# The state-space loop of a two-layer encoder: the first pair of the gated unit is summed whole inside it, and the block outputs share one PSUM bank

## The chip, the cores and the metric

The kernel runs on one core of a Trainium2 chip. The metric is the device time of one execution in microseconds. Before the change, three runs gave a median of 983.5 us (982.42 to 984.84). All arithmetic is float32.

## What is computed

The input is a residual stream of 256 positions by 1024 features. Two layers change it. Layer 0 has an attention and a linear recurrence side by side. Layer 1 has a state-space mixer (S5) with a gated linear unit behind it. Each layer ends in a mixture of 16 experts. The change touches only the S5 mixer of layer 1:

```python
def _s5_mixer(h, ...):
    ...
    bu_re = jnp.einsum('bsgc,gpc->bsgp', u, bb_re)          # inputs of the states
    bu_im = jnp.einsum('bsgc,gpc->bsgp', u, bb_im)
    h_re, h_im = scan(ab, bu)                               # complex diagonal recurrence over the positions
    y = C_re h_re - C_im h_im + d * u
    act = jax.nn.gelu(y.reshape(B, S, D_MODEL))
    zg = act @ glu_w + glu_b                                # (256, 1024) @ (1024, 2048)
    return zg[..., :D_MODEL] * jax.nn.sigmoid(zg[..., D_MODEL:])   # value * sigmoid(gate)

x = x + g_m * m                                             # then norm, router, experts
```

## The kernel before, in words

There are five streams of instructions: TensorE (PE), VectorE (DVE), ScalarE (ACT), GpSimd (POOL), and SyncE (SP), which starts the large transfers. They are held together by counting semaphores. The order on each engine is written out by hand, so an instruction that waits holds back all that stand behind it on its engine. PSUM has 8 banks of 128 by 512 float32, `bank[0]` to `bank[7]`.

**The state-space loop** (PE lines 1843 to 1859, DVE lines 1270 to 1296, ACT lines 840 to 848) runs over `KD` = 8 blocks k of 128 features, and is unrolled. In one turn:

- `states(k + 1)` on PE multiplies the next block's features into the state inputs (L1801, 32 matmuls, banks 0 to 3). It waits until VectorE has read those banks for block k (`s_used`).
- VectorE reads the four banks for block k and turns them by a rotation table (L1277 to L1280), adds (L1282, L1283), does eight scans (L1287), and turns back (L1292 to L1295). The last of these signals `q_ready`. It then takes the next block, for which it waits on `s5_ps`, the signal of `states`.
- `ada(16 + k, 17 + k)` on PE (L1347) multiplies one of eight 2 MB units of the layer's conditioning weights into bank 7. SyncE loads them alternately into ring slots 0 and 1, each when the unit two before it has been used (L350).
- From k = 2 on, `glu_blocks` (L1838) adds to the gated unit what the finished block k - 1 of `actT` gives.
- `outputs(k)` on PE adds up block k of y: the d term (L1815), the direct term (L1816), and, when `q_ready` is k + 1, 64 matmuls from the states (L1823). It signals `y5_ps`.
- ScalarE applies the gelu to it (L842), writes `actT[:, k]`, signals `act_ready`, and makes a later diagonal (L834).

**The gated unit.** The product `act @ glu_w` is cut into eight tiles of 128 positions by 512 columns. A pair m (`GLU_PAIRS`, a column half h and a position half b) consists of a value tile (part 0) and a gate tile (part 1) over the same positions and columns. Each tile is a bias matmul (`glu_bias`, L1830) and 8 block matmuls of 128x128 by 128x512 (`glu_blocks(m, part, lo, hi)`, L1838, blocks lo to hi - 1). Its weights are one of four 2 MB units (`s5_glu_w`, number 2 h + part). Pairs 0 and 1 both use units 0 and 1, pairs 2 and 3 use units 2 and 3.

Before the change the tiles are placed so. The value tile of pair 0 grows inside the loop in bank 6. In the last turn (k = 7) the gate tile of pair 0 is begun in bank 0, with bias and 3 blocks, ahead of `outputs(7)`; 4 more blocks follow behind it, then `ada_cols(2)` (L1357). With block 7 the two tiles of pair 0 are ended. After `gate_row(2)` (L1382) come pairs 1, 2 and 3, each with two whole tiles.

For each pair ScalarE takes the sigmoid of the gate tile (L851), and VectorE multiplies and adds to x (L1302, L1304, L1305). After pair 3 the norm of the mixture of experts begins (L888, L612), its transposes (L1322), router and gathers (L1577), and then four groups of four experts.

**Loads.** SyncE sends, in this order: the rotation tables into slots 4 and 5, conditioning units 16 and 17, gated-unit weights 0 and 1 (L337) into slots 2 and 3, conditioning units 18 to 23, then gated-unit weight 2 (after `q_ready` 4) and weight 3 (after `q_ready` 8), which take the places of the rotation tables. Then it sends the experts' weights of layer 1 (L341), each when its slot's last reader has signalled. For the slots of the gated unit's weights that is the end of a tile of pair 1 (`glu_ps` 3 and 4) or of pair 3 (`glu_ps` 7 and 8).

Of the kernel before, what the change touches and what calls it, by code (L numbers as in the profile page):

```python
# [22 lines left out]
T = 256  # L23
NB = T // P
KD = D // P
# [60 lines left out]
class Chain:  # L86
# [5 lines left out]
    def link(self, ins):  # L92
        ins.then_inc(self.sem, 1)
        self.n += 1
        self.eng.wait_ge(self.sem, self.off + self.n)
# [9 lines left out]
def build(nc, a, out):  # L105
    ctx = ExitStack()
    with ctx:
        def sb(name, shape, dt=F32):
            return ctx.enter_context(nc.sbuf_tensor(name, shape, dt))
# [3 lines left out]
        def S(name):  # L113
            if name not in sems:
                sems[name] = ctx.enter_context(nc.semaphore(name))
            return sems[name]
# [7 lines left out]
        grow = sb("grow", [P, D])  # L124
# [21 lines left out]
        bank = [PS[:, i, :] for i in range(8)]  # L146

        def w3(off, *dims):

            n = 1  # L150
            for d in dims:
                n *= d
            v = work[:, off:off + n]
            if len(dims) == 1:
                return v
            names = " ".join("abcd"[:len(dims)])
            return v.rearrange(f"p ({names}) -> p {names}", **dict(zip("abcd", dims)))
# [41 lines left out]
        gfrow = w3(o, D); o += D  # L199
# [65 lines left out]
                  (1, 0, 1, 4), (1, 1, 1, 5), (0, 0, 1, 7), (0, 1, 1, 4))  # L265
        K0_BANK = (3, 6)
        GLU_PAIRS = ((0, 0), (0, 1), (1, 0), (1, 1))
        GLU_BANK = ((6, 0), (1, 2), (3, 7), (4, 5))

        BATCHES = ((0, ADA_FIRST), (ADA_FIRST, ADA_EARLY), (ADA_EARLY, ADA_ALL))  # L270
        arows = (arow0, arow0, arow1)
# [19 lines left out]
        def loaded(eng, n, i=None):  # L291

            v = 16 * (n // SLOTS + 1)
            if n >= MOE_BASE[1] and (n - ADA_BASE) % SLOTS < 2:
                v -= 16
            eng.wait_ge(S(f"loaded{n % SLOTS}"), v if i is None else v + i * (16 * PER_GROUP // SLOTS))

        def u3(n, c=HALF):
            return ring[:, n % SLOTS, :].rearrange("p (k c) -> p k c", c=c)
# [279 lines left out]
        def _(act):  # L579
# [11 lines left out]
            for name, (at, n) in ROWS.items():  # L591
                dst = rows[at:at + n, :]
# [31 lines left out]

            def gate_row(n):
                act.wait_ge(S("grow_ps"), n + 1)
                at, row = (4, grow) if n % 2 == 0 else (2, gfrow)
                s.activation(row[:, 0:HALF], bank[at], ACT.Copy)
                s.activation(row[:, HALF:], bank[at + 1], ACT.Copy).then_inc(S("grow_ready"), 1)

# [7 lines left out]
            def rows_out(i):  # L638

                act.wait_ge(S("ada_used"), BATCHES[i][1])  # L640
                s.activation(arows[i], bank[7], ACT.Copy).then_inc(S("ada_rows"), 1)
# [188 lines left out]
            def diagonal(k):  # L830

                if k >= 2:
                    act.wait_ge(S("y5_ps"), k - 1)
                s.activation(diagD[:, k % 2, :], ident[:, :], ACT.Copy, scale=col("s5d", k)).then_inc(  # L834
                    S("diag_ready"), 1)
# [4 lines left out]
            for k in range(KD):  # L840
                act.wait_ge(S("y5_ps"), k + 1)
                s.activation(actT[:, k, :].rearrange("p (j l) -> p l j", l=2),  # L842
                             bank[4 + k % 2][:, 0:T].rearrange("p (l j) -> p l j", l=2),
                             ACT.Gelu_apprx_tanh).then_inc(S("act_ready"), 1)
                if k + 2 < KD:
                    diagonal(k + 2)
                if k == KD - 2:
                    rows_out(2)
            for m, (h, b) in enumerate(GLU_PAIRS):
                act.wait_ge(S("glu_ps"), 2 * m + 2)  # L850
                s.activation(q_a[:, m, :], bank[GLU_BANK[m][1]], ACT.Sigmoid).then_inc(S("glu_sig"), 1)  # L851
                if m == 0:
                    gate_row(2)
# [9 lines left out]
        def _(dve):  # L863
# [436 lines left out]
            for m, (h, b) in enumerate(GLU_PAIRS):  # L1300
                dve.wait_ge(S("glu_sig"), m + 1)
                link(v.tensor_tensor(q_a[:, m, :], q_a[:, m, :], bank[GLU_BANK[m][0]], ALU.mult))  # L1302
                dve.wait_ge(S("grow_ready"), 3)
# [13 lines left out]
        def _(pe):  # L1317
# [6 lines left out]
            def bcol(ap, n=P):  # L1324
                return ap.to_broadcast([ap.shape[0], n])
# [25 lines left out]
            def ada_cols(i):  # L1351

                pe.wait_ge(S("ada_rows"), i + 1)
                lo, hi = BATCHES[i]
                n, r = hi - lo, lo % ADA_EARLY
                for c4 in range(4):
                    last = mm(bank[6 if i == 0 else 7][:, c4 * n:(c4 + 1) * n], arows[i][:, c4 * P:(c4 + 1) * P],  # L1357
                              sel[:, r:r + n], start=True, stop=True)
                last.then_inc(S("ada_cols_ps"), 1)
# [16 lines left out]
            def gate_row(n):  # L1376

                L, sec = n // 2, (G_M if n % 2 == 0 else G_F)
                pe.wait_ge(S("mod_cols"), (2, 2, 3, 3)[n])
                at = 4 if n % 2 == 0 else 2  # L1380
                for k in range(KD):
                    last = mm(bank[at + k // 4][:, (k % 4) * P:(k % 4 + 1) * P], bcol(mod[:, L, sec, k:k + 1]),  # L1382
                              ident[:, :], start=True, stop=True)
                last.then_inc(S("grow_ps"), 1)
# [29 lines left out]
            for j in range(LT):  # L1414
                at = 768 + j * P
# [7 lines left out]
            for j in range(LT):  # L1423
                at = 1280 + j * P
# [30 lines left out]
            for b in range(NB):  # L1455
                n_k = P * (b + 1)
                for i in range(4):
                    for r in range(2):
                        h = 2 * i + r
                        if b == 0:  # L1460
                            dst = PS[:, r, i * P:(i + 1) * P]
                        else:
                            dst = PS[:, (4, 2)[r] + i // 2, (i % 2) * T:(i % 2 + 1) * T]
# [341 lines left out]
            def outputs(k):  # L1805

                m = k % 2
                dst = bank[4 + m]
                pe.wait_ge(S("diag_ready"), k + 1)
                if k >= 2:  # L1810
                    pe.wait_ge(S("act_ready"), k - 1)
                else:
                    pe.wait_ge(S("tab_evac"), 12)
                    pe.wait_ge(S("k0_evac"), 2)
                mm(dst[:, 0:T], diagD[:, m, :], hT[:, k, :].rearrange("p (j l) -> p l j", l=2), start=True, stop=False)  # L1815
                mm(dst[:, 0:NJ], K0[:, k, :], hT[:, k, 0::2], start=False, stop=False)  # L1816
                pe.wait_ge(S("q_ready"), k + 1)
                for w in range(4):
                    for l, tab in ((1, H1), (0, H0)):
                        n = NJ - 1 + l  # L1820
                        for q4 in range(4):
                            cc = slice(32 * q4, 32 * q4 + 32)
                            last = mm(dst[cc, NJ:T] if l else dst[cc, 1:NJ], tab[:, w // 2, k, cc],  # L1823
                                      qq[m][:, w, q4 * NJ:q4 * NJ + n], start=False, stop=w == 3 and l == 0)
                last.then_inc(S("y5_ps"), 1)

            def glu_bias(m, part):

                r = GLU_PAIRS[m][0] + 2 * part
                mm(bank[GLU_BANK[m][part]], bcol(ident[0:4, r:r + 1]), glub, start=True, stop=False)  # L1830

            def glu_blocks(m, part, lo, hi):

                h, b = GLU_PAIRS[m]
                n = GLU_BASE + 2 * h + part
                loaded(pe, n)
                for k in range(lo, hi):
                    last = mm(bank[GLU_BANK[m][part]], actT[:, k, b * P:(b + 1) * P], u3(n)[:, k, :], start=False,  # L1838
                              stop=k == KD - 1)
                if hi == KD:  # L1840
                    last.then_inc(S("glu_ps"), 1)
# [3 lines left out]
            for k in range(KD):  # L1845
                if k + 1 < KD:
                    states(k + 1)
                ada(ADA_EARLY + k, ADA_EARLY + k + 1)
                if k == 2:
                    pe.wait_ge(S("glub_in"), 16)  # L1850
                    glu_bias(0, 0)
                if k >= 2:
                    pe.wait_ge(S("act_ready"), k)
                    glu_blocks(0, 0, 0 if k == 2 else k - 1, k)
                if k == KD - 1:
                    pe.wait_ge(S("s_used"), KD)
                    glu_bias(0, 1)
                    glu_blocks(0, 1, 0, 3)
                outputs(k)
            glu_blocks(0, 1, 3, KD - 1)  # L1860
            ada_cols(2)
            pe.wait_ge(S("act_ready"), KD)
            glu_blocks(0, 0, KD - 1, KD)
            glu_blocks(0, 1, KD - 1, KD)
            gate_row(2)
            for m in range(1, 4):
                if m == 3:
                    pe.wait_ge(S("grow_ready"), 3)
                for part in range(2):
                    glu_bias(m, part)  # L1870
                    glu_blocks(m, part, 0, KD)
            pe.wait_ge(S("x_new"), 3)
# [27 lines left out]
```

## Time and profile before

| | us |
|---|---|
| Median of 3 runs | 983.5 |
| The profiled execution, device time | 982.88 |
| Its span | 981.1 |
| TensorE busy | 848.6 (86%) |
| VectorE busy | 304.4 (31%) |
| ScalarE busy | 192.7 (20%) |
| GpSimd busy | 150.6 (15%) |
| State-space loop, from the first L1277 to the last L1295 | 494.9 to 567.2 |
| Gated unit after the loop, to the last sigmoid | 567.4 to 626.7 |

The span is the time from the first to the last instruction that the profile shows. In the rows below, PE is TensorE's matmuls and PEld its weight loads, which overlap them. A float32 matmul appears as two records, so "x16" at L1838 is 8 block matmuls. A row of the timeline says when the group began, how long it took, engine, line and operation, what it writes and reads, how many, and in brackets how long the engine had been idle before it and what ended that.

### The profile page before, as it was taken

To read this page: it belongs to the slowest core of one execution; us is meant where nothing else is said; L and a number is where in the kernel's file an instruction comes from. 1 tells how busy PE (TensorE), PEld (TensorE's weight loads), DVE (VectorE), ACT (ScalarE), POOL (GpSimd) and SP (SyncE) were. 2 spreads that over 40 slices of the span, in tenths; PEclk is the share of its full clock that TensorE was granted. 3 is DMA by queue.
4 is the path that set the end of the run, shared out by engine and by line. 5 is a ranking of instruction groups with operands and counts; after the bars stand their busy time and mean duration, and the time that the engine had idled before them with its cause. 6 is when DMAs were issued, how large, how long until landed. Compare 5 with 4: busy or idle time off the path is not lost.

```text
span 981.1 us, 12755 instructions
## 1 busy us (share of the span) xinstructions
PE 848.6 (86%) x5229; PEld 463.8 (47%) x5230; DVE 304.4 (31%) x708; ACT 192.7 (20%) x311; POOL 150.6 (15%) x244
## 2 busy tenths in 40 slices
PE   3799566979999999899868799789999799999993
PEld 0367352456546455365444454344444464554641
DVE  1320653254113141031389921332000121311314
ACT  1301224042121131121320010211000211312211
POOL 3201002708543434600000000010000000000000
PEclk9799867989999999999999999979999899999997
DMA  9999697533999999999698674404777289999961
GB/s 311 347 382 290 242 358 283 163 113 142 398 393 399 399 396 395 399 391 398 257 387 286 242 276 152 172 1 155 274 257 257 87 326 396 392 399 390 395 267 65
DMA packets 126288, 285.32 MB, mean 291 GB/s; under 512 B 7093, under 2 KB 8389, under 8 KB 125993
## 3 DMA queue, kind: packets, MB, share of 16 engines
q1 hardware_dynamic: 119392, 276.83, 76.7%
q0 software_dynamic: 1984, 5.21, 1.8%
q10 hardware_dynamic: 4872, 2.72, 1.1%
q8 instruction: 29, 0.48, 0.2%
q14 instruction: 11, 0.08, 0.0%
HBM read 279.50 MB, written 5.24 MB: 290 GB/s over the span
## 4 chain that ended last, share of the span: by engine, by line
PE 70%; DVE 12%; DMA 9%; ACT 3%; issue 3%; SPq 2%; DVEq 0%; ACTq 0%
PE PS L1550 17%; PE PS L1569 12%; PE PS L1577 8%; PE PS L1593 7%; PE PS L1553 6%; PE PS L1838 5%; DMA ring<-in_moe_w 5%; PE PS L1322 4%; PE PS L1518 3%; PE PS L1411 3%; DMA work<-in_ada_w 2%; DMA ring<-in_ada_w 2%; DVE work L1287 2%; PE PS L1347 2%; SPq L350 1%
## 5 line engine op out<-in xcount | busy, mean ns | idle before, releaser
L1569 PE MATMUL PS<-ring,work 128*64 128x512 f32 (+1 forms) x512 | 130.5, 597 | 6.2 <-ACT work L768 6.2
L1550 PE MATMUL PS<-ring,hT 128*64 128x256 f32 x896 | 107.5, 381 | 3.7 <-DMA ring<-in_moe_w 3.7
L1550 PE MATMUL PS<-ring,yg 128*64 128x256 f32 x896 | 106.6, 379 | 0.0
L1550 PEld LDWEIGHTS PS<-ring,hT 128*64 128x64 f32 x896 | 66.1, 137 | 41.2 <-issue 7.9
L1569 PEld LDWEIGHTS PS<-ring,work 128*64 128x64 f32 (+1 forms) x512 | 43.1, 143 | 85.4 <-issue 83.9
L1209 DVE TENSOR_TENSOR work<-work,PS 128x512 f32<-128x512 f32 x32 | 22.0, 688 | 194.3 <-PE PS L1550 146.4
L1577 PE MATMUL PS<-work,xhat 128*128 128x256 f32 (+1 forms) x256 | 76.2, 449 | 6.7 <-issue 6.6
L1550 PEld LDWEIGHTS PS<-ring,yg 128*64 128x64 f32 x896 | 67.6, 137 | 29.1
L1213 DVE COPY yg<-PS 128x512 f32<-128x512 f32 x32 | 22.1, 692 | 180.5 <-PE PS L1569 180.5
L1593 PE MATMUL PS<-yg,grow 64*128 64x512 f32 (+1 forms) x256 | 70.1, 612 | 7.1 <-DVE yg L1213 7.1
L1577 PEld LDWEIGHTS PS<-work,xhat 128*128 128x128 f32 x256 | 48.4, 204 | 38.6 <-issue 21.9
L1838 PE MATMUL PS<-ring,yg 128*128 128x512 f32 x128 | 58.9, 604 | 0.0
L1347 PE MATMUL PS<-ring,condz 128*32 128x512 f32 x320 | 41.7, 650 | 14.0 <-DMA ring<-in_ada_w 13.8
L772 ACT ACTIVATE yg<-PS 128x512 f32<-128x512 f32 x32 | 19.1, 597 | 166.5 <-PE PS L1569 166.5
L1593 PEld LDWEIGHTS PS<-yg,grow 64*128 64x128 f32 (+1 forms) x256 | 25.6, 186 | 35.9 <-issue 22.1
L764 ACT ACTIVATE work<-PS 128x512 f32<-128x512 f32 x32 | 19.1, 598 | 104.6 <-PE PS L1550 79.3
L493 POOL TENSOR_SCALAR rt<-rt 128x4 f32<-128x4 f32 x2 | 0.5, 241 | 253.3 <-DVE rti L1170 253.3
L1838 PEld LDWEIGHTS PS<-ring,yg 128*128 128x128 f32 x128 | 23.1, 189 | 33.9 <-issue 33.9
L768 ACT ACTIVATE work<-PS 128x512 f32<-128x512 f32 x32 | 19.1, 597 | 96.4 <-PE PS L1322 96.4
L1322 PE MATMUL PS<-ident,work 128*128 128x128 f32 x176 | 29.3, 288 | 6.7 <-ACT yg L772 6.3
L1518 PE MATMUL PS<-ring,yg 128*128 128x512 f32 x64 | 29.9, 628 | 2.8 <-issue 2.8
L1322 PEld LDWEIGHTS PS<-ident,work 128*128 128x128 f32 x176 | 19.2, 143 | 27.5 <-issue 26.8
(348 smaller groups left out, 968.5 us busy)
## 6 DMA issues: line engine op xcount, KB each, us to landing
ring<-in_moe_w SPq DMA_DIRECT2D x96, 2048.0 KB, 16.5
ring<-in_ada_w SPq DMA_DIRECT2D x20, 2048.0 KB, 14.9
work<-in_ada_w SPq DMA_DIRECT2D x4, 2048.0 KB, 17.1
ring<-in_s_glu_w SPq DMA_DIRECT2D x4, 2048.0 KB, 16.7
ring<-in_ab_w_in SPq DMA_DIRECT2D x3, 2048.0 KB, 22.1
ring<-in_ab_w_out SPq DMA_DIRECT2D x2, 2048.0 KB, 10.0
rot_tables<-work POOLq DMA_DIRECT2D x16, 256.0 KB, 5.8
ring<-rot_tables SPq DMA_DIRECT2D x2, 2048.0 KB, 10.9
```

Of the source, the lines that this page charges most:

```text
L1209: v.tensor_tensor(he[:, e % 2, :], he[:, e % 2, :], bank[1], ALU.mult).then_inc(S("he_ready"), 1)
L1213: v.tensor_copy(yg[:, e % 2, HALF:], bank[3]).then_inc(S("y_dve"), 1)
L1322: return nc.tensor.transpose(dst, src, ident[0:n, 0:n])
L1347: last = mm(bank[7][32 * j:32 * j + 32, :], condz[:, k, 32 - r:64 - r], ada_unit(u)[:, k, :], start=any(first) and k < 4, stop=any(final) ...
L1411: last = mm(dst, w[:, k, :], hT[:, k, :], start=k == 0, stop=k == KD - 1)
L1518: last = mm(bank[2 * b + h], mixT[:, k, b * P:(b + 1) * P], u3(N_WIN + h)[:, k, :], start=k == 0, stop=k == KD - 1)
L1550: last = mm(dst[64 * u:64 * u + 64, 0:256], hg[k][:, e * P:e * P + 64], w[:, k, 256 * u:256 * u + 256], start=k == 0, stop=k == KD - 1)
L1553: last = mm(dst, hg[k][:, e * P:(e + 1) * P], w[:, k, :], start=k == 0, stop=k == KD - 1)
L1569: last = mm(dst, heT[:, at:at + (64 if narrow else P)], w[:, c4, h * HALF:(h + 1) * HALF], start=c4 == 0, stop=c4 == KF - 1)
L1577: last = mm(bank[k % 2].rearrange("p (e n) -> p e n", n=P)[:, :, 0:n_s], xhat[:, b, k * P:(k + 1) * P], pick[:, b, :, 0:n_s], start=b == 0 ...
L1593: last = mm(acc[2 * b + h], pickT[pp, e, b * P:(b + 1) * P], yg[pp, at, h * HALF:(h + 1) * HALF], start=False, stop=False)
L1838: last = mm(bank[GLU_BANK[m][part]], actT[:, k, b * P:(b + 1) * P], u3(n)[:, k, :], start=False, stop=k == KD - 1)
```

## The change

The value and gate tiles of pair 0 are now both summed inside the loop, in banks 6 and 5. In the last turn, where the gate tile of pair 0 was begun, the value tile of pair 1 is begun (bank 0), with bias and 3 blocks, and 4 blocks behind `outputs(7)`. After the loop, block 7 ends three tiles (both of pair 0, the value tile of pair 1). Of pair 1 only the gate tile is left to do whole.

To free bank 5, all blocks' outputs go to bank 4 (before: banks 4 and 5 in turn). So `outputs(k)` waits for the gelu of block k - 1 (before: k - 2). The banks of the other tiles, and those of the gate row after the loop (2 and 3 instead of 4 and 5), are moved to suit.

```diff
-        GLU_BANK = ((6, 0), (1, 2), (3, 7), (4, 5))
+        GLU_BANK = ((6, 5), (0, 1), (7, 4), (2, 3))
...
             def gate_row(n):
...
-                at, row = (4, grow) if n % 2 == 0 else (2, gfrow)
+                at, row = 4 if n == 0 else 2, grow if n % 2 == 0 else gfrow
...
                 s.activation(actT[:, k, :].rearrange("p (j l) -> p l j", l=2),
-                             bank[4 + k % 2][:, 0:T].rearrange("p (l j) -> p l j", l=2),
+                             bank[4][:, 0:T].rearrange("p (l j) -> p l j", l=2),
...
-                at = 4 if n % 2 == 0 else 2
+                at = 4 if n == 0 else 2
                 for k in range(KD):
                     last = mm(bank[at + k // 4][:, (k % 4) * P:(k % 4 + 1) * P], bcol(mod[:, L, sec, k:k + 1]),
...
             def outputs(k):
                 m = k % 2
-                dst = bank[4 + m]
+                dst = bank[4]
                 pe.wait_ge(S("diag_ready"), k + 1)
-                if k >= 2:
-                    pe.wait_ge(S("act_ready"), k - 1)
+                if k:
+                    pe.wait_ge(S("act_ready"), k)
...
                 if k == 2:
                     pe.wait_ge(S("glub_in"), 16)
                     glu_bias(0, 0)
+                    glu_bias(0, 1)
                 if k >= 2:
                     pe.wait_ge(S("act_ready"), k)
-                    glu_blocks(0, 0, 0 if k == 2 else k - 1, k)
+                    for part in range(2):
+                        glu_blocks(0, part, 0 if k == 2 else k - 1, k)
                 if k == KD - 1:
                     pe.wait_ge(S("s_used"), KD)
-                    glu_bias(0, 1)
-                    glu_blocks(0, 1, 0, 3)
+                    glu_bias(1, 0)
+                    glu_blocks(1, 0, 0, 3)
                 outputs(k)
-            glu_blocks(0, 1, 3, KD - 1)
+            glu_blocks(1, 0, 3, KD - 1)
             ada_cols(2)
             pe.wait_ge(S("act_ready"), KD)
-            glu_blocks(0, 0, KD - 1, KD)
-            glu_blocks(0, 1, KD - 1, KD)
+            for part in range(2):
+                glu_blocks(0, part, KD - 1, KD)
+            glu_blocks(1, 0, KD - 1, KD)
             gate_row(2)
             for m in range(1, 4):
                 if m == 3:
                     pe.wait_ge(S("grow_ready"), 3)
-                for part in range(2):
+                for part in range(1 if m == 1 else 0, 2):
                     glu_bias(m, part)
                     glu_blocks(m, part, 0, KD)
```

## Rows read from the trace of the kernel before

**Rows 1.** The page's first line.

```profile
span 981.1 us, 12755 instructions
```

**Rows 2.** The chain that ended last, 460 to 650 us: start, duration, engine, line.

```profile
549.20 0.69 DVE work L1277
...
558.26 1.95 PE PS L1823 x64
...
619.01 7.08 PE PS L1838 x16
626.11 0.61 ACT work L851
...
628.91 1.22 DVE xhat L888
```

**Rows 3.** Stages: stretch, length, busy of PE, PEld, DVE, ACT, POOL, clock, DMA.

```profile
494.00:503.00 9.00, 6.29 (x80) 3.23 (x72) 7.98 (x17) 3.22 (x8) 0.00 (x0) 0.81 1.05 387
...
548.00:557.00 9.00, 6.72 (x118) 4.14 (x118) 8.86 (x19) 0.68 (x2) 0.00 (x0) 1.00 1.05 392
...
577.00:627.00 50.00, 49.07 (x112) 19.69 (x110) 5.81 (x10) 3.15 (x6) 0.00 (x0) 1.00 0.53 190
```

**Rows 4.** Timeline of one settled turn of the loop (outputs of block 4, then 5).

```profile
540.17 1.95 PE L1823 MATMUL PS<-work 128*32 128x128 f32 x64 [1.75 <-DVE work L1295]
...
542.18 0.40 ACT L842 ACTIVATE yg<-PS 128x256 f32<-128x256 f32 x1 [8.37 <-PE PS L1823]
...
542.69 1.19 PE L1801 MATMUL PS<-hT,work 32*128 32x128 f32 x32 [0.57 <-DVE work L1280]
...
545.66 1.12 PE L1838 MATMUL PS<-ring,yg 128*128 128x512 f32 x2
...
546.62 0.61 PE L1815 MATMUL PS<-hT,work 128*128 128x256 f32 x2
...
549.22 1.95 PE L1823 MATMUL PS<-xhat,work 128*32 128x128 f32 x64 [1.75 <-DVE xhat L1295]
```

**Rows 5.** Timeline of the turn k = 2.

```profile
517.52 1.92 PE L1347 MATMUL PS<-ring,condz 128*32 128x512 f32 x16 [0.78 <-DMA ring<-in_ada_w]
...
519.37 1.12 PE L1830 MATMUL PS<-yg,ident 4*128 4x512 f32 x2
...
521.34 0.68 DVE L1295 TENSOR_TENSOR work<-work,ring 128x512 f32<-128x512 f32 x1
...
523.01 1.95 PE L1823 MATMUL PS<-work 128*32 128x128 f32 x64
```

**Rows 6.** Timeline of the turn k = 7 and behind it.

```profile
561.86 1.12 PE L1838 MATMUL PS<-ring,yg 128*128 128x512 f32 x2
...
566.57 0.68 DVE L1295 TENSOR_TENSOR xhat<-work,ring 128x512 f32<-128x512 f32 x1
...
567.42 1.95 PE L1823 MATMUL PS<-xhat,work 128*32 128x128 f32 x64
...
573.64 1.96 PE L1838 MATMUL PS<-ring,yg 128*128 128x512 f32 x4
```

**Rows 7.** Timeline: the gate tile of pair 1 and the start of the next.

```profile
585.43 1.12 PE L1830 MATMUL PS<-yg,ident 4*128 4x512 f32 x2
...
586.48 7.13 PE L1838 MATMUL PS<-ring,yg 128*128 128x512 f32 x16
...
593.55 1.12 PE L1830 MATMUL PS<-yg,ident 4*128 4x512 f32 x2
```

**Rows 8.** Timeline of SyncE's loads of the gated unit's weights: issue times.

```profile
487.19 10.43 SPq L337 DMA_DIRECT2D ring<-in_s_glu_w  x2
...
546.27 21.38 SPq L337 DMA_DIRECT2D ring<-in_s_glu_w  x2
```

**Rows 9.** Issue to landing of conditioning units 16 to 23 (L350).

```profile
DMA to landing us min/median/max: 7.8/11.0/23.0
```

**Rows 10.** The same of the gated unit's weights (L337).

```profile
DMA to landing us min/median/max: 7.9/16.7/19.9
```

**Rows 11.** Waits of TensorE, 649 to 981 us: longest in total, times, longest.

```profile
PE PS L1577 <- issue: 6.6, 2, 4.8
```

## The prediction, made before the changed kernel ran

> **What bounds the kernel now.** I read the chain that ended last first, then the stages, then the timeline of single turns. Up to block 6 the chain through the loop is VectorE's: each turn runs from one L1277 to the next, and from L1277 at 549.20 the chain comes to PE's L1823 at 558.26 [rows 2]. So a settled turn takes 9.05 us (the L1823 at 540.17 and at 549.22 give the same [rows 4]). In a stretch of 9 us VectorE is busy 8.86 us and TensorE 6.72 us [rows 3]. At 558.26 the chain goes over to TensorE and stays there to 626.11, where the last sigmoid starts [rows 2]: from 577 to 627 TensorE is busy 49.07 of 50 us at granted clock 1.00 [rows 3]. After it come three steps of VectorE, and the norm at 628.91 [rows 2]. So two stretches have different owners. In the loop TensorE has free time; behind it every matmul lengthens the kernel.
>
> **How much room TensorE has in a turn.** Before L1823 it is idle 1.75 us for VectorE's last product, and before L1801 0.57 us for VectorE's reads [rows 4]. So a settled turn's TensorE work is 9.05 - 1.75 - 0.57 = 6.73 us.
>
> **The change part by part.**
>
> *1. One more block per turn.* A block alone, with the change to the next kind of matmul, holds the stream 0.96 us (545.66 to 546.62 [rows 4]). What a second one behind it adds: the tile of 8 blocks lasts 7.13 us against 1.12 us for one block, (7.13 - 1.12)/7 = 0.86 us [rows 4, 7]; two blocks last 1.96, that is 0.84 more [rows 6]. I take 0.86; the ends are 0.84 and 1.05 (the distance from the bias to the next group [rows 7], were each change of bank to cost what a change of kind costs). A new turn's work is 6.73 + 0.86 = 7.59 us, under 9.05. Cost on the path in turns 3 to 6: nothing, as VectorE's turn covers it. Were that cover gone, 0.86 us a turn.
>
> *2. The turn k = 2 gets a bias and two blocks more:* 3 x 0.86 = 2.58 us. This turn has no room: VectorE ended L1295 at 521.34 + 0.68 = 522.02, and TensorE came to L1823 only at 523.01 [rows 5], having waited 0.78 us for a conditioning unit and done bias and blocks. Now L1823 starts at 525.59, 3.6 us late. While TensorE is late its idle pieces are gone, so it makes good 9.05 - 7.59 = 1.46 us per turn: L1823 of k = 3 at 533.18 (2.1 late against 522.02 + 9.05 = 531.07), of k = 4 at 540.77 (0.6 late against 540.17 [rows 4]). At k = 5 it is in time again, at 549.22, with some 0.85 us left.
> Does that lateness reach VectorE? VectorE's next turn needs `states`, which TensorE issues right behind L1823. They end 1.95 + 1.19 = 3.14 us [rows 4] after it starts: the states for block 4 at 528.7 (VectorE wants them at 531.1), for block 5 at 536.3 (wanted at 540.15). Margins 2.4 and 3.8 us: VectorE is never held. So TensorE stands at L1823 of block 6 at 558.26 as before, and the loop costs nothing.
>
> *3. The wait for the previous gelu (one bank for all outputs).* Behind the waiting L1815 stand L1816 and L1823, and behind them the next states. The gelu ends at 542.58 and L1815 starts at 546.62, 4.0 us later [rows 4]. From k = 2 on the blocks in front of it wait for the same gelu already. At k = 1, with no block in between, the margin is 0.96 less, some 3.1 us. I take zero; if it bit, it could cost at most the gelu with its signals, 542.69 - 542.12 = 0.6 us a turn, and TensorE's room of 0.87 would still hide that.
>
> *4. From 558.26 on TensorE is the path, and I count what it issues.* Added: one block in turn k = 7 (value and gate take block 6, instead of the value alone) and one at the end (block 7 ends three tiles instead of two): 2 x 0.86 = 1.72 us. The first is not hidden: L1823 of k = 7 starts at 567.42, where VectorE was ready at 566.57 + 0.68 = 567.25 [rows 6], so TensorE was already the later by 0.17 us. Were all of that block hidden the gain would be 0.86 more. Unchanged: bias and 3 blocks in front of `outputs(7)`, 4 blocks behind, only of another tile. Removed: one whole tile of pair 1, bias and 8 blocks, 593.55 - 585.43 = 8.12 us [rows 7]. Net 8.12 - 1.72 = 6.4 us. With 1.05 for a block it is 6.0. The last sigmoid starts at 619.7 instead of 626.11.
>
> *5. Loads.* Weight 1 is now used at k = 2 instead of k = 7. It was issued by 487.19 + 10.43 = 497.6, and the longest landing is 19.9 us [rows 8, 10]: 517.5 at the latest, and it is used behind the biases, after 521. Weight 3 is issued by 567.65 [rows 8] and lands by 587.6. Pair 2's gate tile, three tiles from the end, started at 626.1 - 3 x 8.12 = 601.7 and now starts at 595.3: 7.7 us of margin. The conditioning units are each sent when the one two turns before has been used. The late turns push unit 21 by 2.6 us, 22 by 2.1 and 23 by 0.6. Each has nearly two turns (some 16 us) against a landing of 11.0 us in the median [rows 9]. The worst landing of 23.0 belongs to the crowd at the loop's start, with the tables and gated-unit weights in front. I take zero; a miss costs at most the push, 2.6 us, and VectorE's turn hides it again. The experts' first weights follow the ends of tiles, so they come earlier or keep their distance.
>
> *6. Banks of the tiles and the gate row.* The gate row waits for VectorE's conditioning columns, which three blocks now cover instead of two. No instruction is added. Zero.
>
> *7. Behind the loop.* The whole rest shifts. From 649 to 981 us TensorE waits on no expert weight for long: its longest item of waiting is instruction issue, 6.6 us in two places [rows 11]. What comes later then keeps the 6.4 us.
>
> **Sum.** The span is 981.1 [rows 1], so 974.7; the profiled execution took 982.88, so 976.5. Its median sibling is 983.5, 0.6 above. I predict 983.5 - 6.4 = 977.1.
>
> **The clock.** Granted clock is 0.81 at the loop's start (a mix of the 1.2 and 2.4 GHz levels) and 1.00 in the settled turns, in spite of idle pieces of 1.75 us in every turn [rows 3, 4]. The Trainium skill ("TensorE: Matmul & The Clock Gate", "A second HAM failure mode: psum-queue depth-cycling") tells of a kernel that cycles through banks, micro-idles between its groups and falls back to the lower clock again and again. By that rule two tiles fed alternately could spoil the turns. The trace does not agree for the settled turns as they are, and the change shortens the idle pieces.
>
> **The rivals.**
> - *TensorE's lateness reaches the last turns.* If the added matmuls cost more like 1.1 to 1.3 us (signals, changes of bank), k = 2's lateness is not worked off before k = 7 and up to 2 us of it stand in front of the exclusive stretch, with another 0.5 in it: gain 3.5 to 4.5, 979 to 980. For it: no room at k = 2. Against it: 1.46 us per turn to recover, over four turns. Chance 0.08.
> - *The gain is given back at a fixed point,* a load whose time doesn't depend on the tiles (weight 3, the experts' first ones, the code behind the 6.6 us of issue). Then 982 to 984, no change. Against it: the margins above. Chance 0.05.
> - *More than counted,* 7.3 to 8.5 us (975 to 976.2): the block at k = 7 is hidden, or a clock dip near the norm falls better. Chance 0.08.
> - *Slower: the loop becomes TensorE's.* If the granted clock fell to 1.2 GHz in the turns, up to 7.59 us of work would last twice as long, 15.2 us, against VectorE's 9.05: 6 us a turn. It decides where the turns 3 to 7 grow by more than 6.4/5 = 1.3 us each, i.e. at a mean TensorE turn above 10.3 us. With two such turns the kernel takes 983.5 - 6.4 + 12 = 989. For it: the 0.81 in the first turn. Against it: 1.00 in the settled turns and less idle time now. Chance 0.03.
>
> **How the numbers follow.** Forecast 0.76, rivals 0.08, 0.05, 0.08 and 0.03. The three runs before lie 2.4 us apart, so a median moves by about 1; the forecast's own range is 975.5 to 978.7. The range for 8 in 10 takes in part of the first and third rivals: 974.6 to 979.8. A measurement of this kernel can tell about 0.3%, 3 us, from no change, so faster means below 980.55: 0.90 (forecast, the third rival and most of the first). Same 0.07, slower 0.03.
>
> **What would show it.** Right: VectorE's turns still 9.05 us apart, the last L1295 near 567.2; L1823 at k = 2 near 525.6 and in time again by k = 5; L1823 of k = 7 near 568.3; the last L851 near 619.7; five whole tiles of 8.12 us after the gate row instead of six. Wrong: a turn of more than 9.05 us from k = 3 on, a wait of L1815 on the gelu, a wait of L1838 on a load, a granted clock under 1.00 between 503 and 620, or a stretch from the last sigmoid to the end that differs from before by over 1 us.

## The result, and the profile after

The first comparison gave 974.43 us (4 runs, 973.61 to 975.74) against 982.96 (4 runs). The ratio was 0.9914, 95% interval 0.9892 to 0.9935. The forecast was 977.1 us, 974.6 to 979.8. So the direction was right, and the time lies 0.2 us under the range.

The profiled execution tells another number. It took 975.74 us with a span of 973.9, against 982.88 and 981.1: 7.1 us less. I go through it in the order of the prediction. First the chain that ended last, of the changed kernel (start, duration, engine, line):

```profile
558.03 1.95 PE PS L1823 x64
...
612.38 7.08 PE PS L1838 x16
619.48 0.61 ACT work L851
...
622.29 1.22 DVE xhat L888
```

Against [rows 2] the last L851 comes 6.63 us earlier. Of that 0.24 us was there when the loop began: the first L1277 starts at 494.68, before at 494.92. The kernel before, then the changed one:

```profile
494.92 0.69 DVE L1277 TENSOR_TENSOR work<-PS,ring 128x512 f32<-128x512 f32 x1 [1.45 <-PE PS L1801]
```

```profile
494.68 0.69 DVE L1277 TENSOR_TENSOR work<-PS,ring 128x512 f32<-128x512 f32 x1 [1.45 <-PE PS L1801]
```

The next view is the timeline of TensorE and VectorE:

```profile
519.30 1.98 PE L1830 MATMUL PS<-yg,ident 4*128 4x512 f32 x4
...
521.10 0.69 DVE L1295 TENSOR_TENSOR work<-work,ring 128x512 f32<-128x512 f32 x1
521.21 3.70 PE L1838 MATMUL PS<-ring,yg 128*128 128x512 f32 x8
...
525.51 1.95 PE L1823 MATMUL PS<-work 128*32 128x128 f32 x64
...
530.87 0.69 DVE L1277 TENSOR_TENSOR work<-PS,ring 128x512 f32<-128x512 f32 x1
...
532.96 1.95 PE L1823 MATMUL PS<-xhat,work 128*32 128x128 f32 x64
...
539.92 0.69 DVE L1277 TENSOR_TENSOR work<-PS,ring 128x512 f32<-128x512 f32 x1
...
540.39 1.95 PE L1823 MATMUL PS<-work 128*32 128x128 f32 x64
...
548.99 1.95 PE L1823 MATMUL PS<-xhat,work 128*32 128x128 f32 x64 [0.89 <-DVE xhat L1295]
...
558.03 1.95 PE L1823 MATMUL PS<-work 128*32 128x128 f32 x64 [0.89 <-DVE work L1295]
...
566.34 0.69 DVE L1295 TENSOR_TENSOR xhat<-work,ring 128x512 f32<-128x512 f32 x1
...
568.04 1.95 PE L1823 MATMUL PS<-xhat,work 128*32 128x128 f32 x64
...
569.92 3.70 PE L1838 MATMUL PS<-ring,yg 128*128 128x512 f32 x8
...
574.27 2.82 PE L1838 MATMUL PS<-ring,yg 128*128 128x512 f32 x6
```

These answer to [rows 4 to 6]. VectorE's turns stay 9.05 us apart (530.87, 539.92). VectorE's last product of k = 2 ends at 521.79, and TensorE comes to L1823 at 525.51: 3.7 us late. It is 2.1 late at k = 3 and 0.45 at k = 4. From k = 5 it waits again, 0.89 us a turn, against 1.75 before. The two blocks that stand on the path cost what was summed for them: L1823 of k = 7 comes 0.86 us later than before, counted from the first L1277, and the three blocks at the end take 2.82 us instead of 1.96 [rows 6].

The stages of the changed kernel (busy of PE, PEld, DVE, ACT, POOL, clock, DMA) against [rows 3]: a settled turn has 7.54 us of TensorE instead of 6.72, and behind the loop it is never idle. (Nor was it before: its last matmul ends at 618.94 + 7.13 = 626.07, and the 0.93 us that are missing from the 50 lie behind that.)

```profile
494.00:503.00 9.00, 6.02 (x72) 3.31 (x64) 8.22 (x17) 2.98 (x8) 0.00 (x0) 0.81 1.05 387
548.00:557.00 9.00, 7.54 (x121) 4.52 (x120) 8.86 (x19) 0.67 (x2) 0.00 (x0) 1.00 1.05 394
577.00:618.00 41.00, 41.00 (x105) 17.55 (x104) 6.18 (x9) 2.28 (x4) 0.00 (x0) 1.00 0.62 228
```

I split every execution at two marks, the start of the first L1277 and the start of the last L851. The middle piece holds all that the change touches. "Rest" is from the last L851 to the end of the span.

| profiled execution | span | front | middle | rest |
|---|---|---|---|---|
| before | 981.1 | 494.92 | 131.19 | 354.99 |
| changed | 973.9 | 494.68 | 124.80 | 354.42 |
| difference | 7.2 | 0.24 | 6.39 | 0.57 |

The middle is 6.39 us shorter, where 6.4 was forecast. The other 0.8 us of this pair of profiles is outside it.

### The profile page after: what moved, and what is told of

It is laid out like the page before. It is cut to its first block, busy times and chain, and to the rows that moved or that the text cites. A ratio compares the mean times of both kernels' runs of the same rounds, so it can differ in the third digit from the quotient of the medians.

```text
span 973.9 us, 12755 instructions
## 1 busy us (share of the span) xinstructions
PE 846.3 (87%) x5229; PEld 464.1 (48%) x5230; DVE 305.2 (31%) x708; ACT 192.8 (20%) x311; POOL 150.6 (15%) x244
## 4 chain that ended last, share of the span: by engine, by line
PE 70%; DVE 12%; DMA 9%; SPq 3%; ACT 3%; issue 3%; DVEq 0%; ACTq 0%
PE PS L1550 17%; PE PS L1569 12%; PE PS L1577 8%; PE PS L1593 7%; PE PS L1553 6%; PE PS L1838 5%; DMA ring<-in_moe_w 5%; PE PS L1322 4%; PE PS L1518 3%; PE PS L1411 3%; DMA work<-in_ada_w 2%; DMA ring<-in_ada_w 2%; DVE work L1287 2%; SPq L350 2%; PE PS L1347 1%
## 5 line engine op out<-in xcount | busy, mean ns | idle before, releaser
L1347 PE MATMUL PS<-ring,condz 128*32 128x512 f32 x320 | 41.9, 652 | 14.9 <-DMA ring<-in_ada_w 14.9
```

The source lines that it names most:

```text
L1347: last = mm(bank[7][32 * j:32 * j + 32, :], condz[:, k, 32 - r:64 - r], ada_unit(u)[:, k, :], start=any(first) and k < 4, stop=any(final) ...
```

## The experiments

Ten more runs were profiled behind the first result. The two ends to be told apart: the edit gives 6.4 us and the rest is spread between executions, or it has a second effect of some 2 us elsewhere.

**The changed kernel again.** No edit.

> The changed kernel as it is, to settle the size of the gain. Theory (the edit alone): from the first L1277 to the last L851 it takes 124.8 us against 131.2 before, 6.4 us less, and the rest of the first result (7.2 us between the two profiled executions, 8.5 between the medians) is the spread between executions, from the first loads and from where the clock rises: so some 6.4 to 7.2 us between medians, ratio near 0.993. Rival (the change has a second effect outside the loop): 8.5 us again, ratio 0.9914, and the stretch from the last L851 to the end is shorter than before by the same 1 to 2 us in each profile.

Measured: 976.17 us (7 runs) against 981.82 (18 runs), ratio 0.9942 (0.992 to 0.9964). Middle 124.81, front 494.15, rest 355.44. The middle is the same to 0.01 us, and the rest is longer than before (354.99), not shorter: against the second effect. The 5.7 us between medians are less than the 6.4 to 7.2 that I expected. The edit's 6.4 us lies inside the interval of the ratio (3.5 to 7.9 us).

**One bank alone,** in the kernel before:

```diff
-                             bank[4 + k % 2][:, 0:T].rearrange("p (l j) -> p l j", l=2),
+                             bank[4][:, 0:T].rearrange("p (l j) -> p l j", l=2),
...
-                dst = bank[4 + m]
+                dst = bank[4]
...
-                if k >= 2:
-                    pe.wait_ge(S("act_ready"), k - 1)
+                if k:
+                    pe.wait_ge(S("act_ready"), k)
```

> The kernel before with one part of the change alone: all outputs in bank 4, each waiting for the gelu before it. Theory: 4.0 us lie between a gelu's end and the next L1815, so nothing moves: 131.2 us from the first L1277 to the last L851, 0 us in all. Rival (the wait bites): up to 0.6 us a turn, at most 3 us longer.

Measured: 982.07 us (12 runs) against 981.82, ratio 0.9996 (0.9983 to 1.0009), middle 131.20. The shared bank costs nothing. Its timeline shows, in a settled turn, the distance between the gelu's end (540.91 + 0.40) and the next L1815 (545.35), 4.0 us as read before:

```profile
538.90 1.95 PE L1823 MATMUL PS<-work 128*32 128x128 f32 x64 [1.75 <-DVE work L1295]
...
540.91 0.40 ACT L842 ACTIVATE yg<-PS 128x256 f32<-128x256 f32 x1 [8.37 <-PE PS L1823]
...
545.35 0.61 PE L1815 MATMUL PS<-hT,work 128*128 128x256 f32 x2
```

**Nothing of pair 1 in front of the last outputs.**

```diff
-                if k == KD - 1:
-                    pe.wait_ge(S("s_used"), KD)
-                    glu_bias(1, 0)
-                    glu_blocks(1, 0, 0, 3)
                 outputs(k)
-            glu_blocks(1, 0, 3, KD - 1)
+            pe.wait_ge(S("s_used"), KD)
+            glu_bias(1, 0)
+            glu_blocks(1, 0, 0, KD - 1)
```

> The changed kernel, but nothing of pair 1 in front of outputs(7): its bias and blocks 0 to 6 all come behind L1823 of k = 7. The same matmuls, only later. Theory (from L1823 of block 6 on TensorE is the path, and only what stands in front of VectorE's last product is free): L1823 of k = 7 starts 9.05 us after that of k = 6, with some 2.7 us of idle TensorE in front of it, and the 3.84 us of bias and three blocks come behind: 124.8 + 2.8 = 127.6 us from the first L1277 to the last L851. Rival (the gain is the pair-0 tile alone, wherever the other blocks stand): 124.8.

Measured: middle 127.46 us, 2.66 more than the changed kernel (expected 2.8); 978.59 us in all (one run). L1823 of k = 7 shows where it went:

```profile
558.05 1.95 PE L1823 MATMUL PS<-work 128*32 128x128 f32 x64 [0.89 <-DVE work L1295]
...
567.10 1.95 PE L1823 MATMUL PS<-xhat,work 128*32 128x128 f32 x64 [2.79 <-DVE xhat L1295]
```

TensorE stands idle for 2.79 us, and the same matmuls come behind. So what counts is not which tile is summed in the loop but how little of TensorE's work is left behind VectorE's last product.

**A block more in each of four turns.** The block is summed twice, so this version no longer computes the layer; it is there for its time.

```diff
                     for part in range(2):
                         glu_blocks(0, part, 0 if k == 2 else k - 1, k)
+                    if 3 <= k <= 6:
+                        glu_blocks(0, 1, k - 1, k)
```

> The changed kernel with one block more in each of the turns k = 3 to 6: the gate tile's new block of pair 0 is added twice. It measures the room left in a turn. In the profile after, TensorE is 3.7 us late at L1823 of k = 2, 2.1 at k = 3, 0.5 at k = 4: it makes good 1.6 a turn. Theory (0.86 us a block, VectorE never held): 0.75 a turn is made good, L1823 of k = 6 is 0.7 us late, VectorE's turns stay 9.05 us, and the stretch takes 125.5 us. Rival (a block costs 1.05 or more, or VectorE is held by late states): VectorE's turns grow and the stretch takes 127 us or more.

Measured: middle 125.25 us, 0.45 more than without the four blocks; VectorE's turns 9.05 (one run). The timeline:

```profile
542.56 1.95 PE L1823 MATMUL PS<-work 128*32 128x128 f32 x64
...
550.86 1.95 PE L1823 MATMUL PS<-xhat,work 128*32 128x128 f32 x64
...
559.16 1.95 PE L1823 MATMUL PS<-work 128*32 128x128 f32 x64
```

TensorE's turn is 8.30 us here, against 532.96 - 525.51 = 7.45 in the changed kernel: the block costs 0.85. I had expected 125.5 us. The difference is in the lateness with which the turns begin: 3.5 us at k = 2 here, where I had taken 3.7 from one profile.

**The tile begun in turn 5.**

```diff
                 if k == 2:
                     glu_bias(0, 0)
-                    glu_bias(0, 1)
...
-                    for part in range(2):
-                        glu_blocks(0, part, 0 if k == 2 else k - 1, k)
+                    glu_blocks(0, 0, 0 if k == 2 else k - 1, k)
+                    if k == 5:
+                        glu_bias(0, 1)
+                    if k >= 5:
+                        glu_blocks(0, 1, 0 if k == 5 else k - 1, k)
```

> The changed kernel, but the gate tile of pair 0 begins in turn k = 5 (bias and blocks 0 to 4 there) instead of k = 2. The same matmuls, with less time to work off the lateness. Theory: up to turn 4 TensorE has its 1.75 us of idle as before; at k = 5 six matmuls of 0.86 us, 5.16 less 1.75, make it 3.4 us late at L1823; at k = 6 it makes good 1.6 and is 1.8 us late; VectorE's turns stay 9.05 us, and the stretch from the first L1277 to the last L851 takes 124.8 + 1.8 = 126.6 us. Rival (where the tile begins is of no account): 124.8. Rival (late states hold VectorE): over 128.

Measured: middle 126.88 us, 2.08 more (expected 1.8); VectorE's turns 9.05 (one run). The timeline of L1823 of k = 4, 5 and 6:

```profile
538.43 1.95 PE L1823 MATMUL PS<-work 128*32 128x128 f32 x64 [1.75 <-DVE work L1295]
...
551.20 1.95 PE L1823 MATMUL PS<-xhat,work 128*32 128x128 f32 x64
...
558.63 1.95 PE L1823 MATMUL PS<-work 128*32 128x128 f32 x64
```

VectorE's products end at 547.42 and 556.46, so TensorE is 3.8 us late at k = 5 (3.4 expected) and 2.2 at k = 6. All but 0.1 us of that is in the middle. The same matmuls, all inside the loop, lose a third of the gain, because only one turn is left to work off the lateness. The start at k = 2 matters.

**The changed kernel a third time.** No edit.

> The changed kernel once more, since the first result gave 8.5 us (4 runs each) and the first repeat 5.7 us (7 runs against 18). Theory (6.4 us from the edit, the rest is spread): the stretch is again 124.8 us, the median is 5.5 to 7.5 us under the kernel before. Rival (a second effect of 2 us): 8 us or more.

Measured: 977.41 us (11 runs, 973.36 to 980.7) against 981.7 (17 runs), ratio 0.9949 (0.9931 to 0.9967). Only 4.3 us between medians, under what I expected (5.5 to 7.5), yet the middle of its profiled execution is 124.77, and that one was among the quickest: front 493.28, rest 354.25, 974.13 us in all. So front and rest together move by more than I had allowed, and the next runs look for it.

**Three more profiled executions of the changed kernel** (look a, b and c), to catch one that is high.

> The changed kernel, one profiled look of three. In the repeats 9 of 22 executions of it lie 3 us and more above its fastest, up to 980.7 us, and no profile has caught one. Theory: the stretch from the first L1277 to the last L851 is 124.8 us in every execution, and a high one has its microseconds in front (loads of the first 60 us, where the profiles so far differ by 2.6 us) or behind (TensorE's clock around the first gathers of layer 1, 1.9 us). Rival: a high execution has them inside the stretch, where the lower clock of 1.2 GHz takes hold in the fuller turns.

> The second look, with the same expectations: 124.8 us for the stretch whatever the total, against a stretch that grows with it.

> The third look, with the same expectations: 124.8 us for the stretch whatever the total, against a stretch that grows with it.

Two of three were high:

| changed kernel | device time | front | middle | rest |
|---|---|---|---|---|
| look b | 973.43 | 492.59 | 124.80 | 354.21 |
| look a | 979.59 | 498.65 | 124.81 | 354.34 |
| look c | 978.78 | 495.34 | 124.80 | 356.86 |

The middle is 124.80 or 124.81 in each. Look a loses its 6 us in front of the loop. Some 2 us are lost early: L996 comes at 65.5 us, against 63.3 in look b, and L1016 at 96.7, against 95.0. In the first 66 us TensorE waits 13.5 us for conditioning weights, against 12.7, and its mean granted clock from 20 to 40 us is 0.68, against 0.78. Another 3.7 us are added up to the last L1100 (200.8, against 195.4), in the stretch of layer 0's attention. There the same 8 matmuls run at either level of the clock. Look b, then look a:

```profile
135.80 1.09 PE L1491 MATMUL PS<-hT,work 128*64 128x128 f32 x8
...
137.40 1.09 PE L1491 MATMUL PS<-hT,work 128*64 128x128 f32 x8
...
139.01 1.09 PE L1491 MATMUL PS<-hT,work 128*64 128x128 f32 x8
```

```profile
137.98 1.97 PE L1491 MATMUL PS<-hT,work 128*64 128x128 f32 x8
...
140.92 1.97 PE L1491 MATMUL PS<-hT,work 128*64 128x128 f32 x8
...
143.59 1.09 PE L1491 MATMUL PS<-hT,work 128*64 128x128 f32 x8
```

From 125 to 145 us the mean granted clock is 0.79 in look b and 0.54 in look a:

```profile
125.00:145.00 20.00, 13.46 (x84) 11.25 (x85) 9.91 (x14) 5.95 (x9) 0.00 (x0) 0.79 1.05 387
```

```profile
125.00:145.00 20.00, 11.94 (x56) 9.55 (x56) 11.60 (x18) 2.98 (x5) 0.00 (x0) 0.54 1.05 387
```

Look c loses 2.65 us behind the loop, at the first gathers of layer 1, which follow a stretch of small steps on VectorE. The chain of look b, then of look c:

```profile
642.38 15.56 PE PS L1577 x32
```

```profile
645.17 17.03 PE PS L1577 x32
...
769.01 6.26 PE PS L1577 x16
```

1.47 us there, and 0.88 at 769 (in look b that group takes 5.38). Around the first of them the mean granted clock is 0.74 in look c (640 to 662 us) and 0.83 in look b (638 to 660). In look c the clock also dipped inside the loop, 0.81 from 512 to 521 us, and the middle did not grow: VectorE's turn covers it.

```profile
512.00:521.00 9.00, 7.27 (x114) 4.64 (x115) 8.86 (x19) 0.68 (x2) 0.00 (x0) 0.81 1.05 386
```

It is not the only one. The changed kernel's first repeat has 0.81 in the same stretch, and look a has 0.89 from 503 to 512 and 0.81 from 521 to 530. So has the kernel with one bank alone, whose turns hold the old number of blocks (0.84 from 512 to 521): the second block is not needed for such a dip. In look a it comes at the turn that has no room. L1347 of k = 2 takes 3.26 us there instead of 1.92, and TensorE is 5.6 us late:

```profile
525.07 0.69 DVE L1295 TENSOR_TENSOR work<-work,ring 128x512 f32<-128x512 f32 x1
...
531.38 1.95 PE L1823 MATMUL PS<-work 128*32 128x128 f32 x64
533.26 1.19 PE L1801 MATMUL PS<-hT,work 32*128 32x128 f32 x32
...
534.84 0.69 DVE L1277 TENSOR_TENSOR work<-PS,ring 128x512 f32<-128x512 f32 x1
...
562.01 1.95 PE L1823 MATMUL PS<-work 128*32 128x128 f32 x64 [0.80 <-DVE work L1295]
```

It is in time again at k = 6 only. The states that VectorE wants at 534.84 end at 534.45, so 0.4 us of margin was left, where the first profile had 2.3 (528.58 against 530.87).

**A further version, on top of the change.** In layer 1 the four matmuls that open the experts' accumulators are moved into idle time of TensorE:

```diff
-                open_acc(0)
-                open_acc(1)
+                if L == 0:
+                    open_acc(0)
+                    open_acc(1)
+                else:
+                    open_acc(2)
+                    pe.wait_ge(S("lg_ready"), L + 1)
+                    open_acc(3)
                 pe.wait_ge(S("member_ready"), L + 1)
...
-                open_acc(2)
-                open_acc(3)
+                if L == 0:
+                    open_acc(2)
+                    open_acc(3)
...
+            pe.wait_ge(S("glu_sig"), 3)
+            open_acc(0)
+            open_acc(1)
             pe.wait_ge(S("x_new"), 3)
             aside1 = ffn(1)
```

> A further version of the changed kernel: in layer 1 the four L1620 matmuls that open the experts' accumulators move: two into TensorE's idle 5.6 us while x and its norm are finished (banks 4 and 5, behind the third sigmoid), two behind the router into its wait for VectorE's choice. In the chain after, 3.71 us of L1620 and 2.44 us of issue stand between the rank matmuls and the first gather; VectorE's picks (L1180) end only 0.6 us before L1620 does. Theory: the gathers start when the picks or the branch on narrow_known allow, 1.5 to 2.5 us earlier, and the stretch from the last L851 to the end shrinks by as much; the clock may stay high longer through the transposes, up to 1 us more. Rival (the wait for the branch's code is what counts, and the openers were hidden by the picks): under 0.5 us.

Measured: 975.21 us (6 runs), ratio to the kernel before 0.9937 (0.992 to 0.9954), middle 124.78, rest 354.26: no better than the changed kernel's rest, 354.2 to 354.4 in four of its six profiles. The rival was right. Its timeline:

```profile
640.77 0.17 DVE L1170 TENSOR_SCALAR rti<-rt 128x4 int32<-128x4 f32 x1
...
641.13 1.66 DVE L1180 TENSOR_SCALAR work<-slotv,rt 128x128 f32<-128x128 f32 x8
...
645.51 0.50 PEld L1577 LDWEIGHTS PS<-work,xhat 128*128 128x128 f32 x2 [6.18 <-issue]
```

TensorE's weight loads now idle for 6.18 us of "issue", and the gather starts 4.6 us behind the end of L1170, which writes the number on which TensorE branches. In the changed kernel, with two openers in between, the openers end at 642.11:

```profile
639.50 0.17 DVE L1170 TENSOR_SCALAR rti<-rt 128x4 int32<-128x4 f32 x1
...
644.55 15.39 PE L1577 MATMUL PS<-work,xhat 128*128 128x512 f32 x32 [2.44 <-issue]
```

That is 4.9 us behind L1170 (4.6 to 4.9 in the six profiles), and in both versions the gather starts 25.0 to 25.1 us behind the last L851. So the openers stood in time that passes anyway. What fills that time no run here shows. It is not the price of every branch, for in layer 0 of the changed kernel the first gather, of the narrow kind with 256 columns, starts 2.7 us behind L1170, right behind the openers:

```profile
217.92 0.17 DVE L1170 TENSOR_SCALAR rti<-rt 128x4 int32<-128x4 f32 x1
...
220.81 9.74 PE L1577 MATMUL PS<-work,xhat 128*128 128x256 f32 x32
```

## Why the prediction was right, and where it was wrong

*Parts 1 to 4, the sum.* Right, to 0.01 us: middle 131.19 to 124.80. A second block costs 0.85 (0.86 taken). In the first profile TensorE is 3.7 us late at k = 2 (3.6), in time by k = 5 (as said), 0.89 us are left per turn (0.85), L1823 of k = 7 starts at 568.04 (568.3). A late turn takes 7.45 us, not 7.59, so it makes good 1.60 us instead of 1.46. VectorE is not held in any profile, though in look a only 0.4 us were left. The run with the last turn left empty shows that the path changes hands at VectorE's last product; the tile begun in turn 5 shows that the turns in between are needed to work off the lateness; one bank alone costs nothing.

*The rivals.* "Lateness reaches the last turns" is a true mechanism with the wrong start: it costs 2.08 us when the tile begins at k = 5, and 0.45 with one block more per turn. "Slower, by the clock" had its condition met in part: in three of six profiles of the changed kernel the granted clock is 0.81 to 0.89 in a stretch of the loop, which was also named as a sign of being wrong. The middle did not grow by it, but look a was near the edge. Nothing came back at a fixed point: in the first profile TensorE waits on no gated-unit weight from the loop to 620 us.

*Part 7, and how the numbers follow: the step that failed.* The forecast is 983.5 - 6.4, with 1 us for what a median moves by. The 6.4 holds; the 983.5 and the 1 us were mis-sized. 983.5 came from three runs; over 40 runs the kernel before has a median of 981.8, 1.7 less. The first four runs of the changed kernel, 973.6 to 975.7, were low; over 25 executions its median is 976.1 (973.36 to 980.7). 981.8 - 6.4 would have been 975.4. Of the first 8.5 us, 6.4 are the edit. The remaining 2 are no more than such spread: in the six profiles of the changed kernel front goes from 492.6 to 498.7 and rest from 354.2 to 356.9, and over all executions the medians lie 5.7 us apart. The profiles do not show that the edit moves front or rest; that each moves by more than 1 us by itself, the prediction left out. The forecast ratio, 977.1/983.5 = 0.9935, lies in each of the three intervals measured (in the first at its end). Seen afterwards, a median of a few runs can fall anywhere in some 973.5 to 980.5.

*What stays open.* The changed kernel's executions are more spread than those before (25 with a standard deviation of 2.4 us, 40 with 1.5); 11 of 25 lie 4 us or more above its fastest, 5 of 40 before. The two high ones that were profiled have their time outside the middle, one of them ahead of any changed instruction. By count the difference is more than chance would easily give (about 1 in 200, if the 4 us had been chosen beforehand, which they were not). Whether the change makes high executions more frequent, and how, stays open: no run was made to find out.

## What to carry to other kernels

Find in the chain the instruction at which the path changes hands from a loop's owner to TensorE. Only TensorE's work behind that point is worth moving, and it gains its own duration, less what must be added behind the same point. Room inside a loop adds up over turns: one turn may be overfilled by several microseconds if enough turns with room follow, and if what the loop's owner takes from TensorE next still comes in time. That margin, not the room alone, is the limit: it was 2.3 us in one execution and 0.4 in another. Read a change of a few microseconds between two marks around it in one execution; here the medians of four runs differed by 8.5 us, those of 25 and 40 by 5.7, and the edit is worth 6.4.

## What the runs showed of the hardware

- The piece between two marks, 125 us on four engines with loads under way, repeats to 0.04 us over six executions of the changed kernel (124.77 to 124.81), even with a different granted clock in a turn. The same kernel's total varies by 7 us.
- Changing the PSUM bank between two blocks of the same shape costs nothing that shows: four blocks over two tiles in two banks take 3.70 us (521.21), and so do four of one tile (569.92). From the start of a bias to the start of its first block 1.05 us pass, from block to block 0.86.
- In layer 1 TensorE's first gather starts 4.6 to 4.9 us behind the number on which it branches, with or without matmuls in between. Where the experts' groups change from wide to narrow gathers, the chain has 4.6 to 4.9 us of "issue" (4.72 in look b). In layer 0 the first gather starts 2.7 us behind that number, without a pause of TensorE. That the long ones are the loading of instructions is argued, not shown.
